# The gate projection of a retention layer, turned around: weights stand, tokens move

## The reference

```
proj = h @ w_in;  q, k, v, g = split(proj)              # g: 256 columns of each head
q, k = rotary(q), rotary(k * dk**-0.5)
o, s_new = retention(q, k, v, s0)                       # chunks of 128 tokens
o = rmsnorm(o, norm_g)                                  # over the 256 columns of a head:
                                                        #   o * rsqrt(mean(o*o) + eps) * norm_g
y = (silu(g) * o) @ w_out
```

## Time and profile before

| | |
|---|---|
| median of three timed executions | 1939.61 us (1939.20 to 1942.01) |
| the profiled execution's own time | 1941.5 us |
| its span, first to last instruction | 1939.7 us |
| PE busy, and share of the span | 1837.1 us, 95% |
| DVE / ACT / POOL busy | 1038.2 / 843.0 / 81.2 us |
| mean granted clock of PE | 0.981 of full speed |
| DMA | 214.18 MB, mean 110 GB/s |

### The profile page before, as it was taken

How to read it: one execution, slowest core, us unless ns; L and a number is a source line. 1 busy time by engine, 2 the same in 40 slices (tenths; PEclk the granted TensorE clock), 3 DMA queues, 4 the chain that set the end, 5 groups by cost and what they waited for, 6 DMA issues and landing times. The chain is left out here.

```text
span 1939.7 us, 29431 instructions
## 1 busy us (share of the span) xinstructions
PE 1837.1 (95%) x10935; PEld 1489.8 (77%) x10935; DVE 1038.2 (54%) x1872; ACT 843.0 (43%) x1756; POOL 81.2 (4%) x140
## 2 busy tenths in 40 slices
PE   5899999999999999699999999999999998889998
PEld 2688888888888888577787767888777776666677
DVE  4553535343535343433546345755168888888852
ACT  3743324233333332422435223433267677878720
POOL 2000000000000000000000000010000000000000
PEclk8899999999999999899999999999999999999999
DMA  8221212140404031463424563223232334543252
GB/s 315 82 91 56 91 55 92 52 125 20 145 0 145 24 121 66 158 217 79 133 74 163 181 214 119 79 90 105 76 98 69 90 125 135 152 131 113 69 174 93
DMA packets 184635, 214.18 MB, mean 110 GB/s; under 512 B 45176, under 2 KB 142914, under 8 KB 183505
## 3 DMA queue, kind: packets, MB, share of 16 engines
q1 hardware_dynamic: 170842, 165.80, 28.0%
q0 software_dynamic: 13696, 47.08, 6.3%
HBM read 164.10 MB, written 48.76 MB: 110 GB/s over the span
## 5 line engine op out<-in xcount | busy, mean ns | idle before, releaser
L464 PE MATMUL rt_acc<-rt_w_hi,rt_h_hi 128*128 128x512 f32 x512 | 207.2, 405 | 7.7 <-DVE rt_w_lo L1008 6.8
L466 PE MATMUL rt_acc<-rt_w_hi,rt_h_lo 128*128 128x512 f32 x512 | 201.1, 393 | 0.0
L465 PE MATMUL rt_acc<-rt_w_lo,rt_h_hi 128*128 128x512 f32 x512 | 200.5, 392 | 0.0
L947 DVE TENSOR_TENSOR rt_by_cos<-rt_raw,rt_cos 128x256 f32<-128x256 f32 (+1 forms) x72 | 30.6, 424 | 282.1 <-ACT rt_raw L788 282.1
L2744 PE MATMUL kq_acc<-kq_w_hi,kq_h 128*128 128x512 f32 x384 | 153.7, 400 | 4.8 <-DVE kq_w_lo L2551 4.8
L2745 PE MATMUL kq_acc<-kq_w_lo,kq_h 128*128 128x512 f32 x384 | 150.6, 392 | 0.0
L2747 PE MATMUL kq_acc<-kq_w_hi,kq_h 128*128 128x512 f32 x384 | 150.5, 392 | 0.0
L464 PE MATMUL rt_acc_g<-rt_g_hi,rt_h_hi 128*128 128x256 f32 x512 | 149.2, 291 | 0.0
L799 ACT COPY rt_qk_t<-rt_tr 128x256 f32<-128x256 f32 (+1 forms) x72 | 26.1, 363 | 275.5 <-PE rt_tr L652 275.5
L465 PE MATMUL rt_acc_g<-rt_g_lo,rt_h_hi 128*128 128x256 f32 x512 | 144.6, 283 | 0.0
L466 PE MATMUL rt_acc_g<-rt_g_hi,rt_h_lo 128*128 128x256 f32 x512 | 144.6, 282 | 0.0
(11 more groups left out here) (374 smaller groups left out, 4213.3 us busy)
## 6 DMA issues: line engine op xcount, KB each, us to landing
ro_a_raw<-retained SPq DMA_DIRECT2D x16, 1024.0 KB, 5.9
op_ada<-in_ada_w SPq DMA_DIRECT2D x8, 1024.0 KB, 12.4
rt_w_raw<-in_ret_w_in SPq DMA_DIRECT2D x16, 512.0 KB, 5.0
rt_w_raw<-in_ret_w_in SPq DMA_DIRECT2D x8, 1024.0 KB, 7.9
rt_old<-in_state_ret SPq DMA_DIRECT2D x8, 1024.0 KB, 6.1
rt_g_raw<-in_ret_w_in SPq DMA_DIRECT2D x8, 1024.0 KB, 5.4
out_st_sample<-rt_new POOLq DMA_DIRECT2D x8, 1024.0 KB, 8.1
kq_w_raw<-in_sb_w_in SPq DMA_DIRECT2D x4, 2048.0 KB, 9.1
```

What stands on the lines that cost most here:

```text
L464: nc.tensor.matmul(dst, h_hi[:, k, cols], w_hi[:, k, :], start=k == 0, stop=False)
L465: nc.tensor.matmul(dst, h_hi[:, k, cols], w_lo[:, k, :], start=False, stop=False)
L466: last = nc.tensor.matmul(dst, h_lo[:, k, cols], w_hi[:, k, :], start=False, stop=k == KD - 1)
```

## The change

In pass two the operands of the gate product change places. For the prompt the head's 256 gate columns are cut into two halves u of 128; a half's weights stand, and 512 tokens (n = 0 or 1) move. That makes four products i = 2n + u of 24 matmuls each; one is done in two pieces of 12, in steps 1 to 8 of the pass. The samples move to step 0: two halves, each with 8 pairs of a 128-column and a 64-column matmul. The gate now comes out transposed, [gate column, token]. So DVE multiplies o by rstd before the transposes (`rate`), and after them, straight from PSUM, by the transposed gate and by norm_g (now one number for each partition), into `o_t`: `take_turned` moves from ACT to DVE. norm_g leaves the splitting of w_out. The order of the five turns becomes tiles 0-1, 2-3, samples, 4-5, 6-7 (before: 0-1, 2-3, 4-5, 6-7, samples), and the stores follow it.

```
             def gates(i, ks):                                        # PE, new
+                u, n = i % 2, i // 2
+                dst, cols, part = acc_g[:, i % 2, :], slice(n * NB, (n + 1) * NB), slice(u * P, (u + 1) * P)
+                for k in ks:
+                    nc.tensor.matmul(dst, g_hi[:, k, part], h_hi[:, k, cols], start=k == 0, stop=False)
+                    nc.tensor.matmul(dst, g_lo[:, k, part], h_hi[:, k, cols], start=False, stop=False)
+                    last = nc.tensor.matmul(dst, g_hi[:, k, part], h_lo[:, k, cols], start=False, stop=k == KD - 1)
+            def sample_gates():                                      # PE, new
+                for u in range(2):
+                    dst, part = acc_g[:, 1, u * P:(u + 1) * P], slice(u * P, (u + 1) * P)
+                    for k in range(KD):
+                        nc.tensor.matmul(dst, g_hi[:, k, part], h_hi[:, k, SEQ:SEQ + 2 * NS], start=k == 0, stop=False)
+                        last = nc.tensor.matmul(dst[:, 0:NS], g_lo[:, k, part], h_hi[:, k, SEQ:SEQ + NS], start=False, stop=k == KD - 1)
...
-                    pe.wait_ge(taken_g, freed(h, t, 2))              # PE, pass two
-                    product(nc, acc_g[:, t % 2, 0:DV], h_hi, h_lo, g_hi, g_lo, t).then_inc(projected_g, 1)
+                    if t == 0:
+                        pe.wait_ge(taken_g, h * GATES + 1)
+                        sample_gates().then_inc(projected_g, 1)
+                    elif t % 2:
+                        pe.wait_ge(taken_g, h * GATES + 1 + t // 2)
+                        gates(t // 2, range(0, KD // 2))
+                    else:
+                        gates(t // 2 - 1, range(KD // 2, KD)).then_inc(projected_g, 1)
...
+                        act.wait_ge(projected_g, h * GATES + (i + 3))         # ACT, steps 2, 4, 6, 8
+                        act.wait_ge(o_out, h * TURNS + (3 if i == 3 else 1))
+                        nc.scalar.activation(g_t[:, gate_slot(i % 2, i // 2), :], acc_g[:, i % 2, :], ACT.Silu).then_inc(taken_g, 1)
...
-                nc.vector.scalar_tensor_tensor(o[0:r, t, :], o[0:r, t, :], rstd[0:r, t:t + 1], g[0:r, t % GATES, :],
-                                               ALU.mult, ALU.mult).then_inc(gated, 1)
+                nc.vector.tensor_scalar(o[0:r, t, :], o[0:r, t, :], rstd[0:r, t:t + 1], None, ALU.mult).then_inc(rated, 1)
...
+            def take_turned(h, n):                                   # DVE; on ACT it was one copy
+                m = TURN_ORDER[n]
+                dve.wait_ge(o_turned, h * TURNS + (n + 2))
+                if n == 0:
+                    dve.wait_ge(o_free, h + 1)
+                dve.wait_ge(taken_g, h * GATES + (2 if m == NPT // 2 else 4 if m < 2 else 6))
...
+                        last = nc.vector.scalar_tensor_tensor(dst, src[:, u], gain, by, ALU.mult, ALU.mult)   # for u = 0, 1
...
-            sp.wait_ge(o_out, H * TURNS)                             # SP, last head
-            sp.dma_start(kept[:, :, 0:SEQ], o_t[:, :, 0:SEQ]).then_inc(last_stored, 16)
-            sp.wait_ge(o_out, H * TURNS + 1)
-            sp.dma_start(kept[:, :, SEQ:SEQ + NS], o_t[:, :, SEQ:SEQ + NS]).then_inc(last_stored, 16)
+            for n, cols in ((2, slice(0, NB)), (3, slice(SEQ, SEQ + NS)), (5, slice(NB, SEQ))):
+                sp.wait_ge(o_out, (H - 1) * TURNS + (n + 1))
+                sp.dma_start(kept[:, :, cols], o_t[:, :, cols]).then_inc(last_stored, 16)
...
-                nc.scalar.activation(w_hi[:, slot(n, k), :], w_raw[n][:, k, :], ACT.Copy, scale=ps.ret_g[:, k:k + 1]).then_inc(hi_s, 1)
+                nc.scalar.copy(w_hi[:, slot(n, k), :], w_raw[n][:, k, :]).then_inc(hi_s, 1)
...
-                nc.vector.scalar_tensor_tensor(w_lo[n][:, k, :], w_raw[n][:, k, :], ps.ret_g[:, k:k + 1],
-                                               w_hi[:, slot(n, k), :].bitcast(F32), ALU.mult, ALU.subtract).then_inc(lo_s, 1)
+                nc.vector.tensor_tensor(w_lo[n][:, k, :], w_raw[n][:, k, :], w_hi[:, slot(n, k), :].bitcast(F32),
+                                        ALU.subtract).then_inc(lo_s, 1)
```

More of the change, by code:

```diff
@@ L556, in after, with gate_slot @@
             return h * NT + (CR + t + 1)
[L558 to L563, removed]
+        GATES = 5
+        G_ENDS = {0: 0, 2: 1, 4: 2, 6: 3, 8: 4}
+        TURN_ORDER = [0, 1, NPT // 2, 2, 3]
+        def gate_slot(u, n):
+            return (2 * n + u) % 3
         def freed(h, t, ring):
@@ L1015, in split_g, with rate, merge_gates @@
                                         ALU.subtract).then_inc(g_lo_s, 1)
-            def gate(h, t):
+            def rate(h, t):
                 r = rows(t)
-                dve.wait_ge(taken_g, after(h, t))
-                nc.vector.scalar_tensor_tensor(o[0:r, t, :], o[0:r, t, :], rstd[0:r, t:t + 1], g[0:r, t % GATES, :],
-                                               ALU.mult, ALU.mult).then_inc(gated, 1)
+                nc.vector.tensor_scalar(o[0:r, t, :], o[0:r, t, :], rstd[0:r, t:t + 1], None, ALU.mult).then_inc(rated, 1)
+            def merge_gates(h):
+                dve.wait_ge(projected_g, h * GATES + 2)
+                src = acc_g[:, 1, 0:2 * P].rearrange("p (u c) -> p u c", u=2)
+                nc.vector.tensor_copy(g_s[:], src[:, :, 0:NS]).then_inc(own, own_n.up())
+                dve.wait_ge(own, own_n.now())
+                nc.vector.tensor_tensor(g_s[:], g_s[:], src[:, :, NS:P], ALU.add).then_inc(merged_g, 1)
+            def take_turned(h, n):
+                m = TURN_ORDER[n]
+                dve.wait_ge(o_turned, h * TURNS + (n + 2))
+                if n == 0:
+                    dve.wait_ge(o_free, h + 1)
+                dve.wait_ge(taken_g, h * GATES + (2 if m == NPT // 2 else 4 if m < 2 else 6))
+                src = tr[:, 0, :].rearrange("p (j u c) -> p u j c", j=2, u=2)
+                for u in range(2):
+                    gain = ps.ret_g[:, bass.ds(h * 2 + u, 1)]
+                    if m < NPT // 2:
+                        cols = slice(m % 2 * 2 * P, (m % 2 + 1) * 2 * P)
+                        by = g_t[:, gate_slot(u, m // 2), cols].rearrange("p (j c) -> p j c", j=2)
+                        dst = o_t[:, u, 2 * m * P:(2 * m + 2) * P].rearrange("p (j c) -> p j c", j=2)
+                        last = nc.vector.scalar_tensor_tensor(dst, src[:, u], gain, by, ALU.mult, ALU.mult)
+                    else:
+                        last = nc.vector.scalar_tensor_tensor(o_t[:, u, SEQ:SEQ + NS], tr[:, 0, u * P:u * P + NS], gain, g_s[:, u, :],
+                                                              ALU.mult, ALU.mult)
+                last.then_inc(o_out, 1)
             def head(h, last, first=False):
@@ L1034, in head @@
                         steps(h, NT)
+                    if t == 0 and not first:
+                        take_turned(h - 1, TURNS - 1)
                     rotate(h, t)
@@ L1048, in head @@
                         spread_k(h)
[L1049 to L1055 removed]
+                        merge_gates(h)
                     if t == 3:
@@ L1059, in head @@
                         dve.wait_ge(inverted, h + 2)
-                    elif t == 4:
-                        for u in range(4):
-                            gate(h, u)
-                    elif 4 < t < NPT:
-                        gate(h, t - 1)
+                    elif 4 <= t < NPT:
+                        for u in ((0, 1, 2, 3), (4, 5), (6, 7), (NPT,))[t - 4]:
+                            rate(h, u)
+                    if 6 <= t:
+                        take_turned(h, t - 6)
                     if not last and 4 <= t < 8:
                         split_w(h + 1, t - 4)
-                gate(h, NPT)
+                take_turned(h, 3)
+                if last:
+                    take_turned(h, 4)
             nc.vector.memset(o[NS:P, NPT, :], 0.0)
```

70 lines of the change are left out of this document (23 added, 47 removed).

## The result

The changed kernel takes 1946.2 us (median of seven executions, 1944.42 to 1947.91), the kernel before 1939.61 us beside it on the same chip. The ratio is 1.003, with a 95% interval of 1.0018 to 1.0041: slower by 3.5 to 8 us. Forecast were 1943.3 us and a range of 1938.5 to 1949.5, with "slower" as the likeliest sign. So the sign is right and the time is in the range, but of the 6.6 us by which the median rose the forecast had 3.7. It is 1.2 us above the 1942 to 1945 that the forecast gave its own case. The profiled execution took 1947.91 us of its own, with a span of 1946.2 against 1939.7.

What follows compares the result with a forecast made beforehand. PE was taken as the bound, busy 95% of the span. Prompt's gate -9.4, samples' gate +12.8 and block end +0.3 gave +3.7 us on 1939.6: 1943.3 us, range 1938.5 to 1949.5.

Steps and rivals of the forecast that it cites:

- likeliest sign: Whole kernel: slower 51%, same 41%, faster 8%, with 0.2% (3.9 us) as the border.
- its own case: Whole kernel: the forecast's main case, from 1942 to 1945 us, 57%.
- The samples' term: Samples' gate on PE: 16 pairs at 223.3 ns, 3.6 us against 2.00 in a head, +12.8 us in all.
- The first rival: Samples' gate: narrow pairs don't wait for their loads, +1.9 instead of +12.8 us, 1932.4 us in all; 7%.
- The prompt's term: Prompt's gate on PE: 512-column matmuls at 226.7 ns save 1.18 us in a head, 9.4 us in all.
- the second rival: Prompt's gate: 512-column matmuls run at the next block's 233.3 ns, +5.1 us at most, 1948.4 us; 18%.
- The step on the turns: Transposes on PE: 18 of o in a head before and after, at the same distances, so no change.
- The end of the block: Last matmul to next block: chain to the store 0.5 us later, smaller store 0.2 less; +0.3, from -0.2 to +1.0.
- Rival four: Next block's weights and block end: norm_g's change and early stores give back 1 and 0.5 us, 1941.8 us; 12%.
- norm_g: Weight splits of w_out in the next block: leaving norm_g out gains 0, at most 1 us.
- DVE and the turns: Second turn in each head: DVE finishes the first pair with 1.0 us or more to spare, so PE waits 0.

Runs made afterwards that it cites:

- The first experiment: Changed kernel with the samples' gate made as before (tokens stand, 16 matmuls of 256 columns at step 0), prompt as changed: 1938.31 us, ratio 0.9993.
- the second: Kernel before with only the samples' gate product replaced by the 16 narrow pairs, in step 8, outputs not the reference's: 1954.53 us, ratio 1.0076.
- the wider pairs: Changed kernel with the second matmul of each narrow pair moving 128 columns instead of 64: 1942.82 us, ratio 1.0019.
- the pairs in two steps: Changed kernel with eight of the 16 narrow pairs in step 0 and eight at the start of step 1: 1957.43 us, ratio 1.0101.
- norm_g back: Changed kernel with norm_g in the w_out splits again and a factor of 1.0 in `take_turned`: 1946.27 us, ratio 1.0026.
- samples second: Changed kernel with the samples' product as 16 matmuls of 256 columns, tokens standing, in step 1 behind 12 prompt matmuls: 1936.27 us (0.9976), again 1934.07 us (0.9964).
- samples third: As samples second, but the samples' product behind both halves of the first prompt product, Silu and merge a step later, some PSUM banks changed: 1940.57 us, ratio 1.0001.

## Why the prediction was right, and where it was not

**The sign and its reason: shown.** The samples' product costs more than the prompt's saves. The first experiment takes the one away and the second makes it alone: 7.9 us less between the medians, with 0.7 us a head of a new wait in it, and 14.9 us more for the kernel before.

**The samples' term.** Forecast 3.60 us for step 0, measured 3.57, against 2.00: +1.57 a head, 12.6 in all against 12.8. The first rival wanted 199 ns a pair or less; no pair shows it, the first one (399.07 to 399.30) neither. That the load and not the columns is paid, which the forecast drew from one group of rows, the wider pairs showed, and the load lane with them.

**The prompt's term was mis-sized.** Forecast -1.18 a head; measured 22.69 us for the eight steps against 23.72 before in the same head, -1.03, so 8.2 us in all and not 9.4. The pace of 226.7 ns is right for some steps; others run at 229 to 231. This is a small part of the second rival (233.3). Which step runs at which pace repeats in every head of the changed kernel; what sets it none of the experiments tells.

**One thing was left out.** The step on the turns says that there is no transpose more or less. In a head that is so, but the fifth turn has four transposes now where the samples' had two, and it stands in the next head's first pass: 0.22 us more there, 0.17 less in the second. For one head (from 306 us) the parts are: gate products 26.27 against 25.72 us, +0.55; transposes +0.05; with rounding the +0.63 of a head, 5.0 us in eight, against 3.4 forecast.

**The clock was not foreseen.** The forecast took PE's clock for granted where PE is always busy. Each profile of a kernel with the narrow pairs of 128 and 64 columns (five profiles: the changed kernel twice, only the samples turned, the pairs in two steps, norm_g back) has one or two stretches of 3.4 us at 1.2 GHz in the passes, in the fourth, sixth, seventh or eighth head; the profiles without them (before, samples as they were, wide pairs, samples second twice, samples third) have none. Those of the changed kernel cost 1.6 us each. This is a step missing from the sum, worth 1.6 to 3.2 us, in the range by its width alone. It could be seen beforehand: the pairs of the earlier trace rows, read 1.7 us further on, run into a fall. In four of the five profiles, and at the 40 pairs of all eleven, PE had issued the narrow pairs without a gap, busy all the time; with the pairs in two steps it had issued eight and then waited 0.9 us. So the narrow pairs are shown to bring the fall. That it is for the fewer columns moved is only argued: the wide pairs differ in nothing else, but there is one profile of them, of their fastest execution. The second sign is the median, 3.4 us lower, though on another chip (as ratios to before 1.0019 against 1.003 and 1.0031, with intervals that overlap).

**The end of the block.** Forecast +0.5 for the chain up to the store, measured 3.44 us from the last stream's end to the last store's issue (810.92) against 2.93: right. Forecast -0.2 for the smaller last store, measured 4.33 us from there to the next load against 5.01: -0.7. With rounding -0.2 instead of +0.3, and -0.4 up to the first matmul of the next block. The stop ahead of the next block is 13.69 us, against 14.02 before and 14.5 forecast. Rival four had this sign.

**norm_g.** Forecast 0, at most 1 us gained. Measured no difference in total and 0.7 us in the block between the two profiles. `retained_out` is 1.7 us shorter after the change. The rest of that, by the rows, is the clock: after the pause PE starts at 1.2 GHz in both, but that lasts 5.9 us from the first matmul before and 4.3 after, and 1.6 us less at half clock is worth 0.8. The stretch is as long in both:

```profile
805.40:822.30 16.90, 5.87 (x14) 4.64 (x15) 8.65 (x12) 9.65 (x15) 0.00 (x0) 0.50 0.86 259
```

in the kernel before, and

```profile
811.20:828.10 16.90, 4.44 (x11) 3.55 (x12) 7.10 (x10) 8.02 (x14) 0.00 (x0) 0.50 0.82 250
```

in the changed one. It only began sooner after PE's last work in the changed kernel: 1.6 us after the last turn's start (809.31) against 3.2. The other profiles bear both parts out. Without norm_g in the splits the block takes 202.0 to 202.2 us where PE runs at 1.2 GHz for 2.8 to 3.7 us from its first matmul, 202.3 to 202.6 with 3.9 to 4.3, and 203.8 with 5.7; with norm_g in them it takes 202.88 with 3.2, 203.64 with 4.6 and 204.25 with 5.9. So the clock's part moves from one execution to the next and isn't to be counted for the change; the 0.7 us of norm_g is.

**DVE and the turns.** Forecast no wait at a turn with 1.0 us or more to spare; none was seen in the changed kernel: in the head from 306 us DVE is done with the first pair at 331.04, and the second turn comes at 332.43, 1.4 us later. How thin that cover is the samples-third kernel shows.

**What stays open.** Beside the pace of the prompt steps, and what makes the clock fall, single profiles differ where nothing was changed: the start of the first head lies between 53.2 and 56.3 us in the eleven profiles, and what follows `retained_out` takes 913.2 to 915.5 us. The medians of the changed kernel, 1946.2 and 1946.6, are 6.6 and 6.3 us above the ones of before beside them. The named parts give 5.0 (heads), 1.6 or 3.2 (clock), -0.4 (to the next block) and about -0.7 (norm_g): 5.5 to 7.1.

**How much of it was luck.** The sign came out by the mechanism that the forecast named. But the terms that it had come to 3.9 us measured, against 3.7 forecast, only because two errors cancel: the heads are 1.6 us dearer than forecast, and the way to the next block and norm_g are 1.4 cheaper. The rest, up to 6.6, is the clock that it left out.

## What to carry to other kernels

Before turning a product around, count its weight loads and not its columns: a load that serves 512 moving columns saves a little (227 to 231 ns, against 239 for two matmuls of 256), one that serves 64 or 128 costs its own 112 ns; so turn the large tiles and leave the small one as it is, which with the small tile second made 4.0 and 6.8 us less than before (ratios 0.9976 and 0.9964) out of a change that cost 6.6 and 6.3 as a whole. When a step becomes shorter, look at what it covered on another engine, and move the short step behind a long one; but count also what queues behind its other parts, since one step further the gain was gone. And a PE that is busy all the time doesn't keep its clock by that alone: compare the granted clock stretch by stretch where narrow matmuls come in, and when you take a price from rows, read on to where their stream ends.

## What the runs showed of the hardware

- A pair of matmuls with two loads of 128 x 128 (float32r) takes 223 ns whether it moves 192 or 256 columns. "TensorE: Matmul & The Clock Gate" of the Trainium skill has under "LDWEIGHTS (loading the stationary operand)" that a load takes its columns / 1.2 ns, which is 107 ns for such a load; 223.6 for two, 111.8 each, agrees to 5 ns. With 256 columns moving, a matmul with its load took 119.5 ns, with 512, 227 to 231.
- Behind 16 such pairs of 128 and 64 columns, issued without a gap, the granted clock fell to 0.50 for 3.4 us, in one or two of eight heads. Within 40 of them in a row it fell in each of eleven profiles, and a pair then took 0.43 us. With 128 and 128 columns it wasn't seen, in one profile.
- A plain subtraction of 128 x 512 takes 683 ns on DVE where one with a factor for each partition takes 743, and the rounding copy on ACT 616 against 711 ns with a factor.
